# One elementwise instruction moved from ScalarE to VectorE, and one group of matmuls issued a step earlier, in a two-layer decoder kernel

## The reference, cut to what matters

```
s = einsum('bqhd,bkhd->bhqk', q, k) * scale
logits = where(mask, s + (c_q - c_k), -inf)
p = softmax(logits, axis=-1)
o = einsum('bhqk,bkhd->bqhd', p, v)
x + (o * silu(gate)) @ w_o
```

## Time and profile before

| what | value |
|---|---|
| median of 3 runs | 1573.7 us |
| the profiled execution's own time | 1574.44 us |
| its span | 1572.7 us |
| busy PE / DVE / ACT / POOL | 1529.1 / 1010.7 / 713.1 / 434.0 us |
| second layer's pairs in the trace | from about 770 us on, some 88.4 us each |
| mean granted clock of TensorE | 0.995 of full speed |

### The profile page before, as it was taken

How to read it: one execution, slowest core, us unless ns; L and a number is a source line. 1 busy time by engine, 2 the same in 40 slices (tenths; PEclk the granted TensorE clock), 3 DMA queues, 4 the chain that set the end, 5 groups by cost and what they waited for, 6 DMA issues and landing times.

```text
span 1572.7 us, 23771 instructions
## 1 busy us (share of the span) xinstructions
PE 1529.1 (97%) x8705; PEld 1135.8 (72%) x8705; DVE 1010.7 (64%) x1979; ACT 713.1 (45%) x1412; POOL 434.0 (28%) x336
## 2 busy tenths in 40 slices
PE   6999999999999999999999999999999999998997
PEld 4688888888888874446777777777777777764543
DVE  7478696877869684135465776767676767676311
ACT  4344455544445552121365555555465555545100
POOL 6012222121222101012243425343343425332200
PEclk9999999999999999999999999999999999999999
DMA  9663929466482943223233545364444445475231
GB/s 267 175 191 120 265 73 269 123 188 194 130 246 89 271 174 84 78 87 100 82 95 107 161 161 175 135 199 137 156 137 142 157 161 175 148 235 216 89 131 42
DMA packets 254085, 242.32 MB, mean 154 GB/s; under 512 B 23162, under 2 KB 219962, under 8 KB 253970
## 3 DMA queue, kind: packets, MB, share of 16 engines
q1 hardware_dynamic: 242834, 204.21, 42.5%
q0 software_dynamic: 11136, 36.59, 6.6%
HBM read 212.63 MB, written 95.24 MB: 196 GB/s over the span
## 4 chain that ended last, share of the span: by engine, by line
PE 90%; DVE 5%; ACT 3%; issue 2%; DMA 0%; SPq 0%; POOL 0%; DVEq 0%; ACTq 0%; POOLq 0%
PE psum L1987 46%; PE psum L2011 7%; PE psum L2496 7%; PE psum L2294 5%; PE psum L2317 4%; PE psum L2301 3%; PE psum L2064 3%; PE psum L2256 2%; PE psum L2350 2%; PE psum L1975 2%; PE psum L2134 1%; PE psum L2150 1%; PE psum L2075 1%; PE psum L2162 1%; PE psum L2152 1%
## 5 line engine op out<-in xcount | busy, mean ns | idle before, releaser
L1987 PE MATMUL psum<-arena 128*128 128x252 f32 (+1 forms) x3472 | 815.2, 385 | 4.5 <-ACT arena L921 3.9
L1987 PEld LDWEIGHTS psum<-arena 128*128 128x128 f32 x3472 | 643.1, 191 | 125.8 <-issue 30.5
L1339 DVE TENSOR_TENSOR arena<-arena,psum 128x252 f32<-128x252 f32 (+1 forms) x310 | 130.6, 421 | 205.0 <-PE psum L1987 195.9
L845 POOL TENSOR_TENSOR arena<-arena 128x1024 f32<-128x1024 f32 x64 | 160.7, 2511 | 226.5 <-DMA arena<-k_pages 208.6
L1157 ACT ACTIVATE arena<-psum,arena 128x256 f32<-128x256 f32 (+7 forms) x128 | 93.7, 739 | 117.0 <-DVE arena L1684 116.7
L921 ACT COPY arena<-psum 128x252 f32<-128x252 f32 (+1 forms) x124 | 45.9, 370 | 172.3 <-PE psum L1987 172.2
L2496 PE MATMUL psum<-arena 128*128 128x512 f32 x256 | 114.4, 597 | 0.0
L2011 PE MATMUL psum<-arena 128*128 128x512 f32 x256 | 113.1, 594 | 0.1
L708 POOL TENSOR_TENSOR arena<-arena 128x512 f32<-128x512 f32 x31 | 40.9, 1319 | 257.0 <-issue 127.0
L1166 ACT ACTIVATE arena<-arena 128x256 f32<-128x256 f32 (+7 forms) x128 | 92.4, 770 | 2.1
L2011 PEld LDWEIGHTS psum<-arena 128*128 128x128 f32 x256 | 47.5, 190 | 57.5 <-issue 56.5
(11 more groups left out here) (265 smaller groups left out, 2150.8 us busy)
## 6 DMA issues: line engine op xcount, KB each, us to landing
k_pages<-in_cache_k SPq DMA_DIRECT2D x64, 512.0 KB, 6.5
v_pages<-in_cache_v SPq DMA_DIRECT2D x64, 512.0 KB, 7.2
arena<-k_pages SPq DMA_DIRECT2D x64, 512.0 KB, 3.6
arena<-v_pages SPq DMA_DIRECT2D x64, 512.0 KB, 5.7
arena<-in_w_in_a SPq DMA_DIRECT2D x32, 512.0 KB, 6.9
arena<-in_x_prompt SPq DMA_DIRECT2D x16, 512.0 KB, 5.5
arena<-in_w_kv SPq DMA_DIRECT2D x16, 512.0 KB, 5.6
arena<-in_w_in_b SPq DMA_DIRECT2D x16, 512.0 KB, 7.3
```

The lines of the kernel that those rows point to most:

```text
L845: pool.tensor_tensor(k_ring[:, m % 2], k_ring[:, m % 2], q_all[:, m % S:m % S + 1, :].broadcast_to([P, PAGES, P]), ALU.mult).then_inc(kq_m ...
L1339: dve.tensor_tensor(out, more, bank[n % 2][:, 0:size(u)], ALU.add).then_inc(of.by_dve, 1)
L1987: ins = pe.matmul(bank[n % 2][:, 0:size(u)], w[:, k, :], x[:, k, :], start=(k == 0 and r in (0, 1, 3, 4)), stop=(k == HK - 1), skip_group_ ...
```

## The change

It has two parts. The absolute value of the gate leaves ACT and becomes an instruction on DVE, `gate_abs(p)`, which clears the sign bit of the values read as integers. It stands between `vg_add(p, 13)` and `row_max(p, 2)`; it has the two waits that the instruction on ACT had, and ACT now waits for it. In PE's order `weighted(p, 2)` moves ahead of the unit `vg_n(2)`.

```diff
-        gate_v, ... = Marks(sem("gate_v"), "in", "silu"), ...
+        gate_v, ... = Marks(sem("gate_v"), "abs", "in", "silu"), ...
...
             def gate_ln(p):
-                act.wait_ge(*b_units.taken(vg_b(p, 13)))
-                if p:
-                    act.wait_ge(norm_done, 2 * p + 1)
-                me.chain(act.activation(g_tmp, g_raw, ACT.Abs))
+                act.wait_ge(gate_v.sem, gate_v.at("abs", p))
...
+            def gate_abs(p):
+                dve.wait_ge(*b_units.taken(vg_b(p, 13)))
+                if p:
+                    dve.wait_ge(norm_done, 2 * p + 1)
+                dve.tensor_scalar(g_tmp.bitcast(I32), g_raw.bitcast(I32), 0x7FFFFFFF, None, ALU.bitwise_and).then_inc(gate_v.sem, 1)
...
                 vg_add(p, 13)
+                gate_abs(p)
                 row_max(p, 2)
...
+                weighted(p, 2)
                 vg_n(2)
-                weighted(p, 2)
                 means_n(0, 1)
```

More of the change, by code:

```diff
@@ L412, in build @@
         max_done, pt_v, norm_done, fin_done = sem("max_done"), sem("pt_v"), sem("norm_done"), sem("fin_done")
-        gate_v, gate_half, smp_gate = Marks(sem("gate_v"), "in", "silu"), sem("gate_half"), sem("smp_gate")
+        gate_v, gate_half, smp_gate = Marks(sem("gate_v"), "abs", "in", "silu"), sem("gate_half"), sem("smp_gate")
         prod_set, k_free, lg_set, df_set = sem("prod_set"), sem("k_free"), sem("lg_set"), sem("df_set")
```

## The result

The changed kernel took 1582.9 us in the median of six timed runs (1580.6 to 1589.5), the kernel before 1574.2 in six on the same chip. The ratio is 1.0060 with a 95% interval of 1.0046 to 1.0075, so 7 to 12 us slower. A second series gave 1.0053 (1.0038 to 1.0068). (The ratio is not quite that of the two medians, which are 8.6 us apart here and 9.1 in the second series.) The forecast was 1580.9 us, 7.2 above before, and slower.

The account below looks back on a forecast made before the run. PE was taken to bound the kernel, running nearly without gaps. 1.5 us for the new DVE instruction plus 5.7 us of stalls at `weighted(p, 2)` made 7.2 on a median of 1573.7: 1580.9 us, range 1575.0 to 1585.0.

Parts of the forecast that it names:

- What bounds the kernel: PE, busy 1529.1 of 1572.7 us, runs nearly without gaps; waits put in front of it are lost in full.
- Nothing gained on ACT: Removing the 1.06 us absolute value only lengthens ACT's idle time before `soft(p, 4)`; worth nothing.
- Part one, 0.30 us in each of seven pairs: New DVE instruction starts `row_max(p, 2)` 0.30 us late; no slack to PE in p = 0 to 6: 2.1 us.
- 0.6 us come back at `scores(p, 4)`: PE's existing wait there for DVE's copy takes up 0.6 of the 2.1 us shift, leaving 1.5 us.
- No hit on the new instruction: The new DVE instruction ends before POOL's multiply starts, so none holds it; nothing added for overlapping transfer issues.
- Part two, four stalls of 1.34 to 1.60 us, 5.7 us: In p = 1 to 4, PE's `weighted(p, 2)` waits for `smp_out`, held on DVE by POOL's multiply.
- No other effect of part two: The product's earlier result shortens no PE wait, since DVE's next copy waits for PE's transposes; no further term.
- The sum: 1.5 + 5.7 = 7.2 us slower, giving 1580.9 us for the median.
- the first (no multiply at that place): POOL's multiply comes later and no longer holds DVE before `weighted(p, 2)`: 1575.2 us; chance 0.16 with at most one stall.
- the second: Multiply falls in all six pairs (9.6 us), new instruction takes 1.23 us (4.9): 1588.2; one alone 1584.8 or 1584.3; chance 0.16.
- the third: POOL's multiply holds the new DVE instruction, up to 2.4 us a hit; half the pairs hit gives 1589; chance 0.04.
- the fourth: Faster: last pair's PE waits of 0.9 and 1.6 us, read as held DVE instructions, go; 1570.3 us; chance 0.06.

Follow-up runs that it names:

- the doubling: The kernel before with the absolute value moved to DVE and that new instruction issued twice in a row, PE's order unchanged; ratio 1.0096 (1.0081 to 1.0111).
- part one alone: The kernel before with only the absolute value moved from ACT to DVE, PE's order unchanged; 1576.7 us against 1575.8, ratio 1.0008.
- part two alone: The kernel before with only `weighted(p, 2)` moved ahead of `vg_n(2)` on PE, the absolute value still on ACT; 1581.9 us, ratio 1.0039.

## Why the prediction was right, and where it was not

**What bounds the kernel**: right. Where nothing waited, nothing changed; outside the clock, what the pairs lost came from waits put in front of PE.

**Nothing gained on ACT**: right. Leaving the work out altogether moved the time by 0.07% with an interval that takes in zero, and left the step behind `soft(p, 4)` as it was.

**Part one, 0.30 us in each of seven pairs**: right in place and nearly in size, 0.29 on DVE and 0.28 on PE, where `turn_values(p, 1)` went from 0.96 to 1.24 us behind the transposes (1.26 forecast). It came in p = 7 too. That the path has no slack is shown by the doubling, where the second 0.73 us arrived in full. The slack had to be read from the distance of starts at `turn_values`, since the list of waits showed none.

**0.6 us come back at `scores(p, 4)`**: 0.57 in the profile, but that number is luck. All of it lies in p = 6, and the kernel without an absolute value, in which nothing is shifted there, has the same -0.57 in p = 6. The long wait of that pair in the profile of before was that execution's own. The term is not shown as a shift taken up; had I left it out, the sum would be 7.8. That the shift vanishes in p = 7 was wrong in the first profile (0.28 stayed, with the wait of 0.86 us as long as ever) and nearly came true in the second (-0.22). With part one alone step 3 to 4 shrank by 1.6 there, more than any shift. That wait is for a reduction on DVE, and the instruction ahead of it takes 2.01 us under POOL's multiply in the first profile, and 0.23 with part one alone, where it starts ahead of the multiply.

**No hit on the new instruction**: the weakest step. I looked at the multiply, which starts 0.6 us or more behind `row_max(p, 2)` in that trace, and gave a hit 4 in 100. What opens the door is the transfer issue of 0.57 us ahead of the multiply: where the instruction became ready 0.18 and 0.28 us into it, DVE was not let in before the multiply had ended. An issue that had only just begun did not hold it. Timeline of POOL and DVE of the kernel with two new instructions, p = 5:

```profile
1231.86 0.91 POOL L818 DMA_DIRECT2D arena<-q_rows  x1 [6.19 <-DMA q_rows<-arena]
```
```profile
1231.95 0.70 DVE L1710 TENSOR_SCALAR arena<-arena 128x1032 int32<-128x1032 int32 x1
```

The issue had run for 0.06 us when the first of the two was done, and it was the issue that took longer, 0.91 us instead of 0.57. In p = 0 of the changed kernel's second profile an issue that had run for 0.12 us did not hold DVE either. In 13 profiles of this study, p = 1 to 7, that issue starts between 0.28 us ahead of and 2.37 us behind the moment when DVE has finished unit 13; it was ahead in 4 of 91 pairs, but in only 2 by more than 0.12 us, both in the first profile. So an estimate from these 91 is that one execution in seven to one in three should pay 2.5 us, and that the first profile paid it twice was bad luck. The sentence of the Trainium skill that I had weighed (SBUF — State Buffer, "Who interferes with whom": whoever issues first gets the shared pair for the whole instruction) agrees with the traces where the scaling and the multiply meet (3.20 us for the second when the first was 0.24 us ahead), but in p = 3 the multiply started at 1053.81, after DVE's instruction was ready at 1053.53, and still went first. I added nothing for the port.

**Part two, four stalls of 1.34 to 1.60 us, 5.7 us**: right in mechanism and in the size of one stall. They were four again and 5.8 us in the first profile, though in p = 2, 3, 4 and 6 instead of 1 to 4; five and 7.1 us with part two alone; two and 3.1 in the second profile, below the three to five of the forecast. So the count of four is partly luck: it varies between executions of one kernel. The cause is shown by taking it away: with `smp_out` out of the multiply's reach no stall was left.

**No other effect of part two**: wrong, by 2.1 us. I had said that the product's earlier end gives nothing, since DVE's next copy waits for PE. The reduction between them does not wait: it frees a key block, the load of the next starts a unit earlier, and so does POOL's multiply, which then holds a scaling of weights ahead of `row_max(p, 7)` that it used to follow. Moving that scaling took this cost, 2.1 to 2.6 us in the profiles with part two, to nothing.

**The sum**: 7.2 us forecast, 9.4 and 8.3 measured in the two series, with intervals of about 2.3 us to either side. The terms that I had left out, 2.1 us of step 7 to 0 and a rare held instruction, are at least as large as the difference, which the intervals alone would allow too. So the closeness of the sum says little about its small terms. The parts measured singly (1.0008 and 1.0039) add up to 1.0047, within the interval of the whole.

**The rivals**: the first (no multiply at that place) is refuted by four stalls; the second holds in neither half, as the new instruction took 0.70 us; the third happened, in two pairs of eight, by way of the issue ahead of the multiply; the fourth did not. One reading in the fourth was wrong: the wait of 1.6 us in p = 7 does not go back to a held instruction, since all six of `smp_out` take 0.15 or 0.16 us there. It is their place in DVE's queue, and moving them took the wait away.

## What to carry to other kernels

Where TensorE runs without gaps, a filler between two dependent steps is worth exactly the wait that it covers, and the wait to ask about is the one that isn't there yet: subtract the filler from the start of the dependent step and look at who is still reading its bank. Where two engines hold each other, as VectorE and GpSimd did here, an instruction's price is its length plus the chance that it becomes ready while the other engine is busy; an issue of a transfer counted too when it had been running for 0.18 us or more. An earlier result also starts the transfers that it releases earlier, so look what they will meet. And a term read from a single profile, such as one long wait in one pair, may be that execution's own: compare a second profile before it goes into the sum.

## What the runs showed of the hardware that I had not expected

- A VectorE instruction of 0.70 us that became ready 0.18 to 0.28 us into an issue of a transfer on GpSimd was also held through the multiply that GpSimd started after it: 3.22 and 3.31 us, where the multiply alone takes 2.37. Where the issue had run for 0.06 and 0.12 us it was not held, and the issue took 0.91 and 0.98 us instead of 0.57 or 0.60. Placed where the multiply was mostly running, it took 1.75 to 3.11 us.
- The same two engines hold each other either way: with the scaling on VectorE started 0.24 us ahead, GpSimd's multiply took 3.20 us instead of 2.35; with the multiply ahead, the scaling took 1.8 to 2.8 us instead of 1.22.
- GpSimd's wait for a transfer of a few kilobytes out of its own queue, ahead of the issue that follows it, was 5.1 to 7.8 us in 91 places of 13 profiles, with a mean of 6.5.
